# A hybrid encoder on one core: in its second mixer, turns become products with a diagonal of reciprocals, and three copies change places

## The reference

```python
def diff_attention(...):            # 4 heads, two score matrices each
    s = jnp.einsum('bqhjd,bshjd->bhjqs', qb, k) * (D_HEAD_DIM ** -0.5)
    a = jax.nn.softmax(jnp.where(visible, s, -jnp.inf), axis=-1)
    attn = a[:, :, 0] - lam * a[:, :, 1]
    o = jnp.einsum('bhqs,bshe->bqhe', attn, v)
    return rms_norm(o, head_norm) * (1.0 - lam_init)

def dsa_mixer(...):                 # 8 heads on one latent, top 128 keys of each query
    score = sum over 4 index heads of relu(q_idx . k_idx) * w_h
    _, idx = lax.top_k(score, topk)
    pr = jax.nn.softmax(scores of the chosen keys)
    ctx = pr @ c_sel ; out = ctx @ w_uv
```

## Time and profile before

| | before |
|---|---|
| median of 3 runs | 1944.99 us (1944.96 to 1948.79) |
| profiled execution | 1945.2 us |
| its span, first to last instruction | 1943.4 us |
| PE busy, share of the span | 1907.2 us, 98% |
| DVE busy | 1029.7 us, 53% |
| ScalarE (ACT) busy | 636.5 us, 33% |
| GpSimd (POOL) busy | 288.8 us, 15% |
| granted TensorE clock, mean | 0.997 |

### The profile page before, as it was taken

The page is one execution under the profiler, slowest core; times in us unless marked ns, Lnnn a source line. Parts: engine busy times, 40 slices in busy tenths (PEclk is TensorE's granted clock), DMA queues, the critical chain, the costliest instruction groups (busy, mean ns, idle before and its releaser), DMA issues.

```text
span 1943.4 us, 24210 instructions
## 1 busy us (share of the span) xinstructions
PE 1907.2 (98%) x8964; PEld 1540.4 (79%) x8964; DVE 1029.7 (53%) x1506; ACT 636.5 (33%) x959; POOL 288.8 (15%) x219
## 2 busy tenths in 40 slices
PE   8999999999999999999999999999989999999997
PEld 6888888777888888887888888877657888888885
DVE  5444477674644442347545442269984644442345
ACT  5323222245323222224323222234573332222222
POOL 2000001212300000224000000173243200000225
PEclk9999999999999999999999999999999999999998
DMA  5323323233223332322322332231101323322321
GB/s 175 108 86 103 102 93 109 77 99 93 87 87 100 105 97 97 109 76 92 110 90 88 111 104 94 96 111 66 54 1 44 108 86 108 97 97 97 108 76 54
DMA packets 56731, 179.59 MB, mean 92 GB/s; under 512 B 12145, under 2 KB 12145, under 8 KB 56657
## 3 DMA queue, kind: packets, MB, share of 16 engines
q1 hardware_dynamic: 54656, 173.69, 27.7%
q0 software_dynamic: 928, 3.02, 0.5%
q10 hardware_dynamic: 1088, 2.10, 0.3%
HBM read 175.04 MB, written 3.15 MB: 92 GB/s over the span
## 4 chain that ended last, share of the span: by engine, by line
PE 91%; DVE 4%; POOL 2%; ACT 1%; issue 1%; DMA 0%; POOLq 0%; SPq 0%; DVEq 0%; ACTq 0%
PE ps L1797 57%; PE ps L1815 25%; PE ps L2246 2%; PE ps L1910 1%; POOL sumsq L1276 1%; POOL square L1274 1%; PE ps L2146 1%; PE ps L2164 1%; DVE sm L1004 0%; PE ps L2195 0%; PE ps L1825 0%; PE ps L2179 0%; PE ps L1961 0%; DVE t L529 0%; DVE t L503 0%
## 5 line engine op out<-in xcount | busy, mean ns | idle before, releaser
L1797 PE MATMUL ps<-x_hi,w_hi 128*128 128x512 f32 x1728 | 681.0, 394 | 8.7 <-ACT w_hi L356 7.6
L1797 PE MATMUL ps<-x_hi,w_lo 128*128 128x512 f32 x1728 | 673.6, 390 | 0.0
L1797 PE MATMUL ps<-x_lo,w_hi 128*128 128x512 f32 x1728 | 673.4, 390 | 0.0
L364 DVE TENSOR_TENSOR w_lo<-raw,w_hi 128x1024 fp32r<-128x1024 f32 x310 | 397.3, 1297 | 409.0 <-ACT w_hi L356 403.1
L356 ACT ACTIVATE w_hi<-raw 128x1024 fp32r<-128x1024 f32 x322 | 332.3, 1050 | 340.4 <-PE ps L1815 293.6
L1797 PEld LDWEIGHTS ps<-x_hi,w_hi 128*128 128x128 f32 x1728 | 325.0, 188 | 82.0 <-ACT w_hi L356 7.6
L1797 PEld LDWEIGHTS ps<-x_lo,w_hi 128*128 128x128 f32 x1728 | 325.1, 188 | 68.4 <-issue 2.4
L1797 PEld LDWEIGHTS ps<-x_hi,w_lo 128*128 128x128 f32 x1728 | 324.9, 188 | 68.6 <-DVE w_lo L364 0.8
L1815 PE MATMUL ps<-act_hi,w_hi 128*128 (+1 forms) x720 | 280.3, 389 | 0.0
L1815 PE MATMUL ps<-act_hi,w_lo 128*128 (+1 forms) x720 | 280.1, 389 | 0.0
L1815 PE MATMUL ps<-act_lo,w_hi 128*128 (+1 forms) x720 | 280.1, 389 | 0.0
(11 more groups left out here) (357 smaller groups left out, 1312.9 us busy)
## 6 DMA issues: line engine op xcount, KB each, us to landing
raw<-in_weights SPq DMA_DIRECT2D x322, 512.0 KB, 3.3
h<-in_xT ACTq DMA_DIRECT2D x4, 512.0 KB, 6.9
out<-result SPq DMA_DIRECT2D x4, 512.0 KB, 3.0
p_raw<-in_pT POOLq DMA_DIRECT2D x2, 512.0 KB, 4.0
scratch_u<-u_sc SPq DMA_DIRECT2D x1, 512.0 KB, 6.6
u_grp<-scratch_u SPq DMA_DIRECT2D x1, 512.0 KB, 4.1
scratch_y<-y_grp SPq DMA_DIRECT2D x2, 256.0 KB, 3.1
y_ch<-scratch_y SPq DMA_DIRECT2D x1, 512.0 KB, 3.6
```

What stands on the lines that cost most here:

```text
L364: dve.tensor_tensor(w_lo[:, slot], raw[:, slot], w_hi[:, slot].bitcast(F32), SUB)\
L1797: last = pe.matmul(ps[:, bank], w[:, slot, k], x[:, k], start=(k == 0 and part == 0), stop=(k == KD - 1 and part == 2))
```

## The change

Four things, all in the second mixer.

1. GpSimd no longer multiplies the rows of the sparse units. It makes a diagonal: the identity times a column with the row's reciprocal, 128 x 128 (`diagonal`, into `diag`, four slots laid over `w_qidx`, which is no longer read by then). PE's turn of a sparse unit is no longer a transpose but a float32 product of the block of `sm` with the diagonal, which turns and scales at once.
2. The differential units from 11 on (PE_MIX) are no longer mixed on DVE. The reciprocal and the factor are made as before, GpSimd makes the diagonal of the factor, and PE turns each block by two products into the same bank: `sm[2u]` with the identity, then `sm[2u + 1]` with the diagonal.
3. ScalarE's copy `o_d` goes ahead of the copy of the turned unit. `d_high` and `d_low` come one step earlier.
4. In group 12, the preparing products (and their copies) go ahead of the turn of `dv` (and its copy).

```diff
+PE_MIX = 11
...
+        diag = over("diag", [P, 4, P], free_lo + 8192)
...
+        def diags_before(u):
+
+            return max(0, min(u, D_UNITS) - PE_MIX) + 2 * max(0, u - D_UNITS)
+
...
+                if u >= PE_MIX:
+                    return
                 dve.wait_ge(od_s["mix_step"], 2 * u + 2)
                 one, two = sm[s % len(sm)][:, 0:keys], sm[t % len(sm)][:, 0:keys]
                 dve.scalar_tensor_tensor(out=one, in0=two, scalar=job[:, 3, s:s + 1], in1=one,
...
-                if k - 2 in D_TURNS:
-                    for i in D_TURNS[k - 2]:
+                if k - 1 in D_TURNS:
+                    for i in D_TURNS[k - 1]:
                         d_low(i)
...
+            def diagonal(u):
+
+                if u == PE_MIX:
+                    pool.wait_ge(od_s["qidx_done"], 2)
+                if u >= PE_MIX + 2:
+                    pool.wait_ge(od_s["turned"], u - 1)
+                if u < D_UNITS:
+                    pool.wait_ge(od_s["mix_step"], 2 * u + 2)
+                else:
+                    pool.wait_ge(od_s["c_recip"], u - D_UNITS + 1)
+                for s in (2 * u, 2 * u + 1)[:1 if u < D_UNITS else 2]:
+                    pool.tensor_tensor(diag[:, s % 4], ident[:],
+                                       job[:, 3, s:s + 1].to_broadcast([P, P]), MULT)\
+                        .then_inc(od_s["diag"], 1)
+
...
-            for u in range(D_UNITS, UNITS):
-                pool.wait_ge(od_s["c_recip"], u - D_UNITS + 1)
-                for s in (2 * u, 2 * u + 1):
-                    buf = sm[s % len(sm)][:, 0:keys_of(u)]
-                    pool.tensor_tensor(buf, buf, job[:, 3, s:s + 1].to_broadcast([P, keys_of(u)]),
-                                       MULT).then_inc(od_s["c_normed"], 1)
+            for u in range(PE_MIX, UNITS):
+                diagonal(u)
...
+                    d_out(k - 4, False)
                     turned(k - 2)
-                    d_out(k - 4, False)
                     exps(k)
                     d_out(k - 4, True)
             for k in range(Z_GROUPS, GROUPS):
+                d_out(k - 4, False)
                 turned(k - 2)
-                d_out(k - 4, False)
                 if k < UNITS:
                     exps(k)
                 d_out(k - 4, True)
+                for number in C_PREP_AT.get(k, ()):
+                    c_prep(number)
                 if k == Z_GROUPS:
                     values_in(3)
-                for number in C_PREP_AT.get(k, ()):
-                    c_prep(number)
...
-                if k - 1 in D_TURNS:
-                    for i in D_TURNS[k - 1]:
-                        d_high(i)
+                for i in D_TURNS.get(k, ()):
+                    d_high(i)
...
+                    bank = 5 + u % 2
+                    for kb in range(blocks):
+                        cols = slice(kb * QB, (kb + 1) * QB)
+                        one, two = sm[2 * u % len(sm)], sm[(2 * u + 1) % len(sm)]
+                        if u < PE_MIX:
+                            last = pe.transpose(ps[:, bank, cols], one[:, cols], ident[:])
+                        else:
+                            pe.matmul(ps[:, bank, cols], one[:, cols], ident[:],
+                                      start=True, stop=False)
+                            last = pe.matmul(ps[:, bank, cols], two[:, cols], diag[:, 2 * u % 4],
+                                             start=False, stop=True)
                 else:
-                    pe.wait_ge(od_s["c_normed"], 2 * (u - D_UNITS) + 2)
+                    pe.wait_ge(od_s["exp"], 2 * u + 2)
+                    pe.wait_ge(od_s["diag"], diags_before(u + 1))
                     pe.wait_ge(od_s["turned_copied"], u)
-                    jobs = [(2 * u + n, 5 + n) for n in range(2)]
...
+                    for s in (2 * u, 2 * u + 1):
+                        for kb in range(blocks):
+                            cols = slice(kb * QB, (kb + 1) * QB)
+                            last = pe.matmul(ps[:, 5 + s % 2, cols], sm[s % len(sm)][:, cols],
+                                             diag[:, s % 4], start=True, stop=True)
...
             for k in range(Z_GROUPS, GROUPS):
                 group(k)
+                for number in C_PREP_AT.get(k, ()):
+                    c_prep(number)
                 if k == Z_GROUPS:
                     values_in(3)
-                for number in C_PREP_AT.get(k, ()):
-                    c_prep(number)
```

More of the change, by code:

```diff
@@ L332, in encoder @@
             "index_step", "sel_step", "dv_turned", "dv_read", "scores", "masked", "exp", "mix_step",
-            "mixed", "turned", "turned_copied", "pv", "c_prep", "c_prep_read", "c_recip", "c_normed",
+            "mixed", "turned", "turned_copied", "pv", "c_prep", "c_prep_read", "c_recip", "diag",
             "c_hi", "c_lo", "d_raw", "d_step", "d_std", "d_rstd", "d_scaled", "d_turned",
@@ L2153, in turn @@
                 if u < D_UNITS:
-                    pe.wait_ge(od_s["mixed"], u + 1)
                     if u >= 2:
                         pe.wait_ge(od_s["turned_copied"], u - 1)
-                    jobs = [(2 * u, 5 + u % 2)]
-                else:
-                    pe.wait_ge(od_s["c_normed"], 2 * (u - D_UNITS) + 2)
+                    if u < PE_MIX:
+                        pe.wait_ge(od_s["mixed"], u + 1)
+                    else:
[5 more added lines that the diff above has]
+                        one, two = sm[2 * u % len(sm)], sm[(2 * u + 1) % len(sm)]
+                        if u < PE_MIX:
+                            last = pe.transpose(ps[:, bank, cols], one[:, cols], ident[:])
+                        else:
+                            pe.matmul(ps[:, bank, cols], one[:, cols], ident[:],
+                                      start=True, stop=False)
+                            last = pe.matmul(ps[:, bank, cols], two[:, cols], diag[:, 2 * u % 4],
+                                             start=False, stop=True)
+                else:
+                    pe.wait_ge(od_s["exp"], 2 * u + 2)
+                    pe.wait_ge(od_s["diag"], diags_before(u + 1))
                     pe.wait_ge(od_s["turned_copied"], u)
-                    jobs = [(2 * u + n, 5 + n) for n in range(2)]
[L2162 to L2165, removed]
+                    for s in (2 * u, 2 * u + 1):
[3 more added lines that the diff above has]
+                                             diag[:, s % 4], start=True, stop=True)
                 last.then_inc(od_s["turned"], 1)
```

## The result

The changed kernel takes 1954.9 us (median of six, 1952.4 to 1956.1) where the kernel before, beside it on the same chip, took 1945.8 (six, 1944.9 to 1948.8): a ratio of 1.0040, 95% interval 1.0030 to 1.0050. It is slower by 9 us, and outside the range. The profiled execution is the slowest of the six, 1956.1 us; the three with the highest mean granted clock, 0.997, took 1952.4, 1952.6 and 1954.2 us, so even they lie above 1952.0.

A forecast was written before the change was run, and what follows sets the result against it. The prediction took TensorE (PE) as the bound, busy 1907 of 1943.4 us. Added passes of 13.5 us less 10.2 us of removed waits gave +3.3 us, so 1948.5 us, range 1945.3 to 1952.0.

The forecast's parts named there:

- stage B: Groups 12 to 18: 4.9 us of passes added, 3.1 us of gaps gone, 0.7 us wait for `dv`; forecast +1.8.
- the price of the port: Units 11 to 15: their five diagonals contend with DVE, between 0 and 1.9 us; taken as 0.
- Stage D: Groups 25 to 29: 3.1 us of passes added, 2.5 of 3.6 us of waits removed net; forecast +0.6.
- Stage C: Groups 19 to 24: 2.0 us of passes fill PE's waits while ScalarE is full; forecast 0.
- the floor of the range: Low end of the range, from rival (2): +0.5 us with passes at 0.107 us, given as 1945.3 us.
- the price of a pass: PE: 0.11 us a pass, float32 product two passes, transpose one; 122 added passes cost 13.5 us.
- stage A: Groups 7 to 11: two waits for `o_d` go, 1.2 us each, so PE reaches group 12 2.4 us sooner.
- stage E: Groups 30 to 33, PE the only full engine: 3.5 us of passes added, 0.2 removed; forecast +3.3.
- Rival (1): B and D: DVE and the diagonals hold PE up, about +5 to +7 us, 1950 to 1952; chance 0.33.
- Rival (2): Groups 7 to 33: all gaps close and nothing new waits, +1.0 us, 1946; chance 0.17.
- rival (4): Gaps stay and passes are simply added; only 3.6 us of `o_d` waits go, +9.9 us, 1955; chance 0.06.

The follow-up runs named there:

- after: The changed kernel itself, with all four parts, run beside the kernel before: 1954.9 us.
- a2: Changed kernel with only the reorders (parts 3 and 4); mixes stay on DVE, sparse scaling on GpSimd, turns stay transposes: 1948.3 us.
- a3: Changed kernel without the mixes on PE (PE_MIX = 16), so differential units are mixed on DVE; sparse diagonals kept: 1951.8 us.
- a4: Changed kernel without the sparse units' diagonals, which GpSimd multiplies and PE transposes as before; mixes on PE kept: 1952.0 us.
- b1: Kernel before with one edit, ScalarE's copy `o_d` ahead of the copy of the turned unit: 1950.0 us.
- a1: Changed kernel with GpSimd's last `w_lo` moved behind the diagonal of unit 12: 1951.3 us.
- c1: a1 with `d_high` and `d_low` put back one step later, where they stood before the change: 1951.4 us.
- d1: b2 with the preparing products (`c_prep`) also ahead of the turn of `dv` on PE and ScalarE: 1945.0 us.
- d3: Changed kernel with one DVE selection step, the one with the scan, moved behind the scaling of `dv`; `w_lo` at its old place: 1951.7 us.
- b2: b1 with GpSimd's last `w_lo` also waiting until DVE has mixed unit 12: 1947.0 us.
- c2: a1 with part 4 undone, the turn of `dv` again ahead of the preparing products: 1954.5 us.
- d2: d1 with one DVE selection step, the one with the scan, moved behind the scaling of `dv`: 1947.3 us.

## Why the prediction was wrong

**The failed step is the term of stage B, "3.1 us of gaps are gone" with "0.7 us of wait" for `dv`, and under it the price of the port, "between 0 and 5 x 0.38 = 1.9 us on DVE; I take 0".** The mechanism was named there, by the very row of 1.21 us, but it was put on the wrong partner. I priced the small diagonals that the change adds; the operation that collided was a `w_lo` of 2.36 us that the change does not touch. I moved PE 2.4 us ahead and left everything that waits for PE where it was. The earlier trace rows had the start of `w_lo` at 1392.10; less the lead of 2.4 that is 1389.7, just ahead of DVE's scan, which began at 1390.39. That was readable and was not asked. It cost 2.1 us of PE's wait (2.8 instead of 0.7); the stage came out at +5.9 us where the sum had +1.8.

**The clock was not in the sum at all**: 1.7 us. Every window of the earlier trace rows showed 1.00, and the new wait came with a fall in all five kernels that had 2.8 us or more of it (after, a2, a3, a4, b1), while a1, c1 and d1 with 0.7, d3 with 1.7, and b2 and c2 with 2.4 had none behind theirs. That is one profiled execution of each, so that the wait brings the fall is likely and not shown.

**Stage D**, forecast +0.6, came out +1.6. The waits for GpSimd and `act_lo` went, as written, and PE's waits on masks did not come. Instead the diagonal of unit 25 met the 512-key scan, 1.4 us; c1 shows that the earlier `d_low` set this up. **Stage C**, forecast 0, came out +0.5.

The account of the 9.0 us: the forecast's 3.3, plus 2.1 and 1.7 in B and 0.3 there that no run assigns, 1.0 in D, 0.5 in C, 0.2 in E, less 0.1 in A. a1, which lacks only the collision in B and the fall, is +5.3. Two slips of the prediction's arithmetic matter to none of this: the floor of the range, +0.5 on 1945.0, is 1945.5 and not 1945.3, and the bounds of A and B in the earlier trace rows are late as said above.

**Right were:** the price of a pass. The turn of the eight blocks of unit 28 begins at 1462.32 and the next at 1464.30 (changed kernel, PE), 1.98 us for 16 passes and what starting the group takes:

```profile
1462.32 2.05 PE L2197 MATMUL ps<-diag,sm 128*128 128x128 f32 x16
1464.30 1.14 PE L2228 MATMUL ps<-pt_c,v_h 128*64 128x128 f32 x12
```

So float32 costs two passes where the transpose costs one; the factor four of the Trainium skill, TensorE: Matmul & The Clock Gate, section Terms, is not what these rows show, since by it the eight blocks would be 32 passes, as an estimate 32 x 0.11 = 3.5 us. Right too were stage A (-2.5 for -2.4; the waits for `o_d` gone, group 12 at 1389.98 less the 1.7 us lost earlier) and stage E (+3.5 for +3.3, PE busy 28.57 of 28.57).

**The rivals.** Rival (1), DVE and the port hold PE up, had the direction and the kind of cause, with 0.33, but its two prices (1.9 in B, `d_low` ahead of two masks in D) were not the ones that were paid, and it ended at 1952. Its rule, the Trainium skill's SBUF - State Buffer, section Who interferes with whom, that whoever issues second waits, agrees with the four collisions shown: `w_lo` first and the scan 3.04 for 0.96, `w_lo` first and the comparison with a number 2.42 for 0.42, the scan first and the diagonals 2.02 for 0.76, the scan first and the multiplies 2.89 for 1.61. In the last two GpSimd lost about 0.3 us more than the rest of the scan, which no run explains. The same section counts `tensor_scalar`, which this comparison is, among the operations that can take DVE's shared port although they have only one whole input; d3's row agrees. Rival (2), all gaps close, fell with B; rival (4), only the `o_d` gaps go, came to the time that was measured (1955) by a way that did not happen: PE's recorded idle time in B to D fell from 7.9 us to 4.6.

## What to carry to other kernels

Where one engine gets ahead, list what it releases on the other engines and see what each of these will then run beside; the longest of them is the risk, not the smallest that the change adds. Price such a collision by what is left of the instruction that is there first, at worst its whole length, and cure it by moving the long instruction beside instructions that it does not hold up (a1: maxima and replacements), not by shuffling its victims (d3). A pass moved to PE is paid in full where PE is the bound (E), and elsewhere gives back only the wait that truly ends last: 122 passes cost 13.5 us here, and even with the collision in B out of the way the change lost 5.3, while three reorders without any pass (d1) won 1.7 in the mixer.

## What the hardware showed that was not expected

The granted clock falls to one half (1.2 of 2.4 GHz) for 3 to 4 us at a time, and each such fall cost 1.7 us: within 1396 to 1400 us in the changed kernel, 1444 to 1448 in b1, 1426 to 1432 in b2, 422 to 428 in the first mixer. A fall is not a fixed consequence of a wait, nor is a long wait needed: in b2 it came behind waits of 0.4 and 0.6 us in C. In the first mixer PE waits 2.0 us for `zq` at 421 us in the kernel before and in the changed one alike, in identical code; the clock fell behind it in five of the thirteen profiled executions (after, b1, b2, d1, d3) and not in the others. This is part of why runs of one kernel spread over 3 us: of the 23 runs of the kernel before in the last set, the twelve with a mean clock of 0.997 took 1945.8 us on average, the ten with 0.996 took 1947.0, the one with 0.995 took 1947.8. It is not all of it, since three of the twelve took over 1947.3. It makes a gain of 2 us in the mixer hard to tell in the total. Whether the falls in C and D of a2, a4, b1 and b2, which keep PE's many short waits for GpSimd, come more often than in the kernel before stays open: the profiles show them in one execution of each, and d1 and d2, which keep these waits too, had none there.
